# Expert combine of a PEER layer: which groups the gathered rows are dealt to, which gathers wait for a gate, and when each output tile is scaled

## The reference, cut to what matters

```python
def expert_chunk(args):
    xc, ic, gc = args                       # token rows, expert indices, softmax gates
    act = gelu(einsum('cd,chkd->chk', xc, u_experts[ic]))
    wgt = gc * act
    return einsum('chk,chkd->cd', wgt, v_experts[ic])
...
x = x + gate2 * peer_ffn(h2, ...)
return rmsnorm(x, g_final)                  # the output, (1, 512, 1024)
```

## Time and profile before

| | us |
|---|---|
| median of 3 runs (lowest, highest) | 1969.96 (1963.08, 1975.21) |
| the profiled execution | 1967.47 |
| its span, first to last instruction | 1965.6 |
| first matmul of the combine | 1414.7 |
| last matmul of the combine ends | about 1950.7 |
| PE busy, share of the span | 1860.4 (95%) |
| DVE busy, share of the span | 1532.8 (78%) |

### The profile page before, as it was taken

One profiled execution on the slowest core, in us unless ns is written; L12 is line 12 of the kernel. 1 busy time (PEld: TensorE's weight loads), 2 busy tenths in 40 slices (PEclk: granted clock), 3 DMA queues, 4 the chain that ended last, 5 costly groups with the idle time before them and its releaser, 6 DMA issues. The chain is left out here.

```text
span 1965.6 us, 27970 instructions
## 1 busy us (share of the span) xinstructions
PE 1860.4 (95%) x10180; PEld 1628.9 (83%) x10180; DVE 1532.8 (78%) x2281; ACT 723.2 (37%) x969; POOL 774.7 (39%) x485
## 2 busy tenths in 40 slices
PE   5999979999899899989999999999989999999996
PEld 5888767777778888889999999999868888888885
DVE  7656367775447588999884599999778888888888
ACT  3322234444333322323333356655532333333331
POOL 0000096000041002557787677878443434333330
PEclk9999989999999999989999999999999999999998
DMA  8899277878482352669999989999999999999993
GB/s 303 281 312 331 89 211 225 250 222 268 155 283 65 69 106 50 154 178 244 275 248 267 265 243 304 302 325 317 334 391 390 391 390 391 390 391 389 391 392 126
DMA packets 305207, 526.24 MB, mean 268 GB/s; under 512 B 20282, under 2 KB 210283, under 8 KB 300524
## 3 DMA queue, kind: packets, MB, share of 16 engines
q1 hardware_dynamic: 268268, 391.10, 64.7%
q0 software_dynamic: 36864, 134.23, 19.7%
HBM read 438.75 MB, written 85.99 MB: 267 GB/s over the span
## 5 line engine op out<-in xcount | busy, mean ns | idle before, releaser
L123 PE MATMUL u_s<-h_hi,u_hi 128*128 128x384 f32 x1024 | 354.6, 346 | 23.8 <-POOL u_lo L1943 19.8
L125 PE MATMUL u_s<-h_hi,u_lo 128*128 128x384 f32 x1024 | 345.3, 337 | 0.0
L124 PE MATMUL u_s<-h_lo,u_hi 128*128 128x384 f32 x1024 | 345.1, 337 | 0.0
L123 PE MATMUL v_o<-v_v_hi,v_w_hi 128*128 128x512 f32 x768 | 301.8, 393 | 11.3 <-DVE v_w_lo L2197 6.7
L124 PE MATMUL v_o<-v_v_lo,v_w_hi 128*128 128x512 f32 x768 | 301.2, 392 | 0.0
L125 PE MATMUL v_o<-v_v_hi,v_w_lo 128*128 128x512 f32 x768 | 301.1, 392 | 0.0
L1943 POOL TENSOR_TENSOR u_lo<-u_ut,u_hi 128x1024 fp32r<-128x1024 f32 x79 | 196.8, 2492 | 100.9 <-ACT u_hi L1723 100.8
L123 PEld LDWEIGHTS u_s<-h_hi,u_hi 128*128 128x128 f32 x1024 | 194.0, 189 | 35.6 <-POOL u_lo L1943 22.3
L124 PEld LDWEIGHTS u_s<-h_lo,u_hi 128*128 128x128 f32 x1024 | 194.7, 190 | 0.0
L125 PEld LDWEIGHTS u_s<-h_hi,u_lo 128*128 128x128 f32 x1024 | 194.2, 190 | 0.0
L1395 POOL DMA_INDIRECT rows_buf<-in_u_experts_dram,few_idx x111 | 155.2, 1398 | 70.8 <-DMA v_gt<-expert_gates 48.7
(11 more groups left out here) (346 smaller groups left out, 4105.8 us busy)
## 6 DMA issues: line engine op xcount, KB each, us to landing
u_raw<-in_u_experts_dram SPq DMA_DIRECT2D x160, 256.0 KB
v_raw<-in_v_experts_dram SPq DMA_DIRECT2D x74, 512.0 KB
v_slot<-in_v_experts_dram SPq DMA_DIRECT2D x54, 512.0 KB
expert_acts<-u_ao SPq DMA_DIRECT2D x64, 384.0 KB
u_raw<-turned_experts SPq DMA_DIRECT2D x96, 256.0 KB
expert_gates<-u_gs SPq DMA_DIRECT2D x12, 2048.0 KB
v_gt<-expert_gates SPq DMA_DIRECT2D x30, 768.0 KB
w_in_raw<-in_w_in_dram SPq DMA_DIRECT2D x17, 1024.0 KB, 11.5
```

The costliest lines, as they stand in the source:

```text
L123: nc.tensor.matmul(out, w[0], x[0], start=first, stop=False)
L124: nc.tensor.matmul(out, w[0], x[1], start=False, stop=False)
L125: return nc.tensor.matmul(out, w[1], x[0], start=False, stop=last)
```

## The change

Three edits in `phase_combine` and its helpers:
1. `adds_by` deals the 160 rows over groups 1 to 30: 160 x min(g, 30) // 30, which is five, five and six rows in turn. Group 31 gets none.
2. POOL waits for the gates of its group in groups 1 to 3 only (PACED = 3). From group 4 on only the ring of eight buffers holds a gather back.
3. `finish(i)` runs right behind `total(i)` for tiles 0, 1 and 2.

```diff
+PACED = 3
 def adds_by(g):
-    return (NSLOT + LATE) * g // (NE // P // GT - 1) - late_by(g)
+    last = NE // P // GT - 2
+    return (NSLOT + LATE) * min(g, last) // last - late_by(g)
 ...
             for g in range(1, NG):
-                pool.wait_ge(sem[f"gt_in{g % 2}"], 16 * (g // 2) + 16 * (g % 2))
+                if g <= PACED:
+                    pool.wait_ge(sem[f"gt_in{g % 2}"], 16 * (g // 2) + 16 * (g % 2))
 ...
             total(0, p_a[:, :])
+            finish(0)
             for i in range(DT - 1):
                 dve.wait_ge(sem["mm"], 2 * DT * (NG - 1) + 2 * i + 2)
                 total(i + 1, p_o[i][:, :])
-                finish(i)
+                finish(i + 1)
 ...
-                if h == 0:
-                    finish(last - 1)
```

## The result

The changed kernel takes 1971.86 us (median of 20 runs, 1966.03 to 1979.61), the kernel before 1966.85 us (20 runs, 1962.22 to 1975.21). The ratio is 1.0022, 95% interval [1.0012, 1.0033]: 2.4 to 6.5 us slower, clear of the scatter and far within 1%. The profiled execution took 1974.01 us with a span of 1972.1 us, where the one of before had 1967.47 and 1965.6.

A forecast was written before the change was run, and what follows sets the result against it. In the combine, PE and DMA (391 GB/s) were taken as both full. Group 31's start at 1934.5 plus 5.6 delay, plus 27.2 for the end, gave span 1967.3, 1.7 slower; scaled to 1972 us, range 1961 to 1982.

The forecast's parts named there:

- delay of PE: Combine stream: rows sent ahead of value tiles make PE late by 5.6 us, between bounds 3.1 and 8.1.
- Bound and limit: Combine, 1500 to 1900 us: PE and DMA both full, 391 GB/s being DMA's limit.
- The end: Combine's tail on DVE: last half tile begins 3.9 us earlier relative to group 31's start; 4.2 us at most.
- S: Start of group 31 on PE: 1934.5 us in the kernel before, forecast as 1934.5 plus PE's delay.
- the case named as the most that can be gained: Tail: DVE keeps its full 3.4 us before group 31, tile 1 still waits for PE; gain at most 4.2 us.
- The lower bound: PE's delay from bytes at group 30: last tile lands at 1917.0 instead of 1912.2, PE late by 3.1 us.
- Group 3: Rows 15 to 17 no longer wait for gate 4: 4 us on top of PE's 4.27 us wait there.
- stream is not pushed: Rival, chance 0.27: rows ahead ride on spare DMA capacity, group 31 starts unchanged at 1934.5, tail gives 3.9: 1966 us.
- the tail gives nothing: Rival, chance 0.03: PE's delay is as forecast and tile 1 waits for PE anyway: 1975 us.
- clock falls: Rival, 0.05 in full, 0.15 in part: PE waits at nine six-row groups lower its clock; up to 1990 or 2000 us.
- The self-limiting: Argument against the clock rival: PE that lost time waits less next group, so the loss partly replaces the wait.
- What would show it right: Signs: gathers wait for adds only; PE waits 4 to 8 us more; matmuls end 1954 to 1959; DMA at 391 GB/s.

The follow-up runs named there:

- after_again: The changed kernel profiled once more, nothing changed; one run, first matmul to last instruction 558.5 us, against 557.0 in the first profile.
- rows150: The changed kernel with 150 gathered rows instead of 160, five in each of groups 1 to 30; ratio to the kernel before 0.9991 [0.9979, 1.0004].
- deal_only: The kernel before with edit 1 alone (rows dealt over groups 1 to 30; all gates, old finish); ratio to before 1.0013 [0.9997, 1.0028].
- deal_finish: The changed kernel with all gates kept (edits 1 and 3, without edit 2); ratio to the kernel before 1.0018 [1.0001, 1.0035].
- gates_off: The kernel before with edit 2 alone (gates in groups 1 to 3 only; old deal, old finish); ratio to before 1.0009 [0.9993, 1.0025].
- ring5: The changed kernel with a ring of five buffers instead of eight; ratio to the kernel before 1.0003 [0.9985, 1.0020].
- offload: The kernel before with scaling moved from DVE to GpSimd and ACT, DVE keeping the last tile's second half; ratio to before 1.0018 [1.0002, 1.0035].
- act_square: The kernel before with sums of squares on ACT (last tile: first half), tile 2 finished inside the last root's wait; ratio 0.9966 [0.9953, 0.9979].

## Why the prediction was right, and where its sizes were not

- **The number: in part luck.** 1972 was forecast and 1971.86 measured. But the forecast stood on a median of 1969.96 of three runs, and 20 runs have 1966.85, which is 3.1 us less; the delay of PE was put too small, which hides it. What the reasoning gave was the difference: 1.7 us slower forecast, 2.4 to 6.5 measured.
- **Bound and limit: right.** At 391 GB/s DMA has nothing in hand for this mix of transfers; over 1500 to 1900 us all thirteen profiles have 390 or 391, while single stretches of 4 us go from 352 to 420 (after_again). rows150 moved the start of group 30 by 6.6 us, and two executions of the changed kernel with different waits in group 3 meet again at group 28 to 0.1 us.
- **The end: right, to 0.2 us.** S + 27.2 was forecast, S + 27.0 measured in both profiles; the last half tile at S + 19.7 against 1964.59 - 1945.1 = 19.5. Which of its two cases would hold was wrong, though. The sum goes by low weights 0.3 us before S, with DVE never waiting for PE; they came 4.1 us before S, and it was the case named as the most that can be gained, with tile 1 waiting for S + 5.4. The two lie 0.3 us apart, so the number did not suffer. I had not said that edit 3 has so small a part in it: 0.7 us, by deal_only and deal_finish.
- **The delay of PE: the term that was mis-sized.** I took 5.6 us between 3.1 and 8.1; it was 10.7 in the profile, and 10.2 or 11.7 (the second execution) counted from the first matmul. Three parts:
  1. The lower bound was read at group 30. Its own number held: landing at 1917.0 forecast, 1917.5 measured. But group 30 is not the one that decides. Group 28 was worse, and a delay of PE there is kept to the end, since PE never runs faster than 16.32 us a group. A bound has to be taken over all groups, and the largest counts; so there was no reason to go below 8.1.
  2. In group 28 all eight rows were ahead, not seven. POOL had issued 152 gathers when ACT got the last tile, the last of them 8.5 us earlier; before it had issued 145, the last of them only 1.0 us earlier. The last tile came 11.0 us later than before, counted from the first matmul (1891.48 - 1415.14 against 1880.11 - 1414.72), and 8 x 1.34 = 10.7. Less 1.2 of slack that gives 9.5, and PE's start of group 28 was 9.8 later.
  3. What a group takes longer behind a wait was left to a rival and not put into the sum: 0.4 us after the wait of 1.57 us, 2.0 us after that of 2.35. Only the second is clock (0.64 over 4 us); the 0.4 came at a granted clock of 1.00, and what it is stays open.
- **Sum.** With a delay of 10.2 instead of 5.6 the same arithmetic gives 6.3 us slower by the profile. The timed ratio says 2.4 to 6.5 us, where I had forecast 1.7. The sign, the place and the mechanism hold; the amount was too small, for the reasons above.
- **Group 3: right in one of two.** 4 us on top of the 4.27 were forecast; the wait was 8.13 us, and 6.06 in the second execution.
- **The rival *stream is not pushed*: wrong**, by the stream distances of all kernels with edit 1 or 2. **The rival *the tail gives nothing*: wrong**, the end is 4.1 us shorter.
- **The rival *clock falls*: right in kind, small in size.** The late waits came in four groups, not in nine, and not in front of the six-row groups but in front of the ones behind them (16, 22, 25, 28). The self-limiting that I named against it is seen: after a loss there is no wait for some groups.
- **What would show it right.** The gathers wait for DVE's adds, yes. The matmuls end at 1961.4, not at 1954 to 1959. DVE starts the last half tile 3.2 us behind them, with 3 to 4 foretold. PE's waits grew by 9.5 us, not by 4 to 8. The granted clock from 1500 to 1900 us stayed at 1.00 as rounded there.

## What to carry to other kernels

Where DMA and TensorE are level, a transfer that is moved ahead of others is paid in full by the ones behind it (11.0 us for eight rows here, 10.7 by their bytes). Moving work away from the end is then an exchange at about the same price, and only what goes ahead of the last transfer that is waited for leaves the end at all. A slack seen on one engine may be the lead of another. The end gets shorter only by work that leaves the engine that is last, for one that does not slow it: here ACT, not GpSimd. And compare profiles by distances between two marks of the same execution, and look for the worst group, not the last.

## What the runs showed of the hardware

- **A wait of PE of about 2 us sometimes costs as much again, and its length does not say when.** What the group behind a wait took beyond 16.32 us: in front of group 2 ten profiles have waits of 1.81 to 1.94 us, of which six cost 1.9 us and four (deal_only, deal_finish, gates_off, ring5) 0.3. Behind the 1.84 us the granted clock was 0.61 over 4 us, so most of these 4 us at the 1.2 GHz level, and the group took 1474.40 - 4.27 - 1451.90 = 18.23 us; behind the 1.86 us of ring5 it was 1.00. Later in the stream 2.35 and 2.58 us cost 2.0, but 2.12 us (ring5) cost 0.4, as all waits up to 1.62 us did, at a granted clock of 1.00. In front of groups 3 and 4, waits of 4.27 to 9.78 us cost 1.78 to 3.11, the longest of them 1.85. What decides between the two outcomes no run here shows.
- **DVE with two SBUF inputs lasts until POOL's instruction ends**, however small its own: 2.38 us instead of 0.16 in offload, in one of four such places. ACT's square beside DVE slowed neither (act_square).
- **Scatter of what lies before.** The first matmul of the combine lay between 1411.3 and 1420.0 us in thirteen executions, the stream of the four kernels that do not push it within 0.9 us, that of the changed kernel in two executions 1.5 us apart.
